# Router rows read back and turned on VectorE, expert tables read one expert ahead, routing by counted rivals

## The chip, the cores and the metric

The kernel runs on one core of one Trainium2 chip. The metric is the time of one execution on the device, in microseconds. Everything is computed in float32.

## The reference, cut to what matters

Two layers run over 2048 tokens of 1024 channels. Each layer adds a mixer (sliding-window attention, pooling and retention behind one RMS norm), and then a mixture of 32 experts behind a second RMS norm. The router takes the two best experts inside the best of eight groups of four.

```python
def moe_ffn(h, router_w, router_b, w_gate, w_up, w_down):
    ...
    scores = jax.nn.sigmoid(jnp.dot(hf, router_w))
    biased = (scores + router_b).reshape(t, N_EXPERT_GROUPS, EXPERTS_PER_GROUP)
    group_score = lax.top_k(biased, 2)[0].sum(-1)
    _, g_idx = lax.top_k(group_score, 1)
    in_group = jnp.take_along_axis(biased, g_idx[:, :, None], axis=1)[:, 0]
    _, local = lax.top_k(in_group, TOP_K)
    ...
for l in range(DEPTH):
    ...
    x = x + jnp.einsum('bse,ed->bsd', mix, w_out[l])
    x = x + moe_ffn(rms_norm(x, norm_ffn[l]), router_w, router_b, w_gate[l], w_up[l], w_down[l])
```

## The kernel before

**Two stages per layer.** The mixer stage goes through the 16 tiles of 128 tokens in a software pipeline of 18 steps (`steps`). In step s a tile s is projected (`front`), tile s-1 is mixed and its new x made (`back`), and tile s-2 is routed (`tail`). Steps 2 to 15 have all three parts, step 16 has `back` and `tail`, step 17 has `tail` alone. The expert stage then goes through the 32 experts in order of their load, with a fixed width of tokens for each (168 down to 128, `WIDTHS`), in groups of at most 32 tokens per quarter of the partitions (`GROUPS`: 6, 5 or 4).

**What sets the order.** Every engine has its own program, written out by hand; the engines meet at semaphores. The sync engine (SP) issues almost all direct DMAs in one queue of its own, in program order, and waits in that queue (`wait_alone`). GpSimd (POOL) issues the indirect DMAs: it scatters each tile's slots into `table` in DRAM, gathers the rows of an expert (L634), and adds the results into `out` (L641).

**The router in the mixer stage.** The new x of tile s-1 is finished on VectorE (DVE) at the end of step s (`x_new`, L966). SP stores it to `out` (L450). In the next step TensorE (PE) turns the eight 128x128 blocks of it into the PSUM banks bA and bB (`tr`, shown by the trace as part of L1154, semaphore `pe_h2T`), and DVE multiplies them by the norm's gain into `h2T` (L897, two instructions). PE then makes the router's partial products (L1275), ScalarE (ACT) copies them (`logits4`, L724), PE folds them (L1286), and ACT takes the exponential (L727). DVE runs `route`: it finds the best group and the two best experts with `first_of` (maximum, compare with a descending code, maximum, compare: L978 to L984), once on 8 groups and twice on 32 experts. PE counts ranks (L1198, L1199), and DVE's `place` writes the slots (L1033 to L1046).

**The final tile.** In step 17 nothing else is left to run. Its chain is PE's turns, DVE's L897, the norm (`norm_2`: L806 to L859, then the rows `h2n` by L864), `route`, ranks, `place`, the scatter, the table's first rows (L471, L472), their gather (L618) and PE's turns of those rows (L1366).

**The expert stage.** For expert i, SP waits for the gate and up products of expert i-2 (`gu_done`), then reads expert i's part of the table (L491, four DMAs), and then starts its weights (L457, L463). POOL waits for that table (L629), issues the gathers of expert i, and then the adds of expert i-2; it waits until the adds have landed before it goes on. DVE's `x_in` turns the gathered rows of expert i+1 (L1099, L1102) before it makes the hidden values of expert i (L1132, L1134, L1137), which PE's down products (L1403) wait for. PE's gate and up products are L1375.

## Time and profile before

| | |
|---|---|
| median of 3 runs | 3338.16 us (3337.02 to 3342.19) |
| the profiled execution | 3337.25 us |
| its span in the trace | 3335.4 us (1.85 us lie around it) |
| PE matmul busy | 3189.2 us, 96% |
| DVE busy | 1535.5 us, 46% |
| POOL busy | 1233.5 us, 37% |
| ACT busy | 590.2 us, 18% |
| mean granted TensorE clock | 0.978 |

The span begins with layer 0's mixer stage (to about 889 us) and its expert stage (to about 1660 us), and layer 1 follows in the same way (mixer to about 2551 us, experts to the end). A fully staffed mixer step takes about 50.7 us, an expert 21.4 to 27.4 us. Of the 146 us in which no matmul runs, most lie at the seams: at the end of each layer's mixer stage, between the two layers, and at the start and the end.

### The profile page before, as it was taken

The page shows a single profiled execution, that of the slowest core. Times are in us where ns is not written, and L with a number is a line of the kernel's source. Part 1 is how long each engine was busy: PE and PEld are TensorE (multiplying, and loading weights), DVE is VectorE, ACT ScalarE, POOL GpSimd, SP SyncE. Part 2 cuts the span into 40 slices and gives each one's busy share as a digit, 9 for nine tenths or more (in the row PEclk, how much of TensorE's full clock was granted, in tenths as well). Part 3 has the DMA queues.
Part 4 walks back from the last instruction along what each step waited for, and adds up shares of the span by engine and source line. Part 5 has one row for each costly group of instructions (what it writes and reads, how often), then busy time and mean ns, then how long its engine had stood idle before and what let it go on. Part 6 is the DMA issues. An engine that isn't in the chain of part 4 may idle for free.

```text
span 3335.4 us, 60077 instructions
## 1 busy us (share of the span) xinstructions
PE 3189.2 (96%) x20372; PEld 2502.4 (75%) x20372; DVE 1535.5 (46%) x4768; ACT 590.2 (18%) x1746; POOL 1233.5 (37%) x1346
## 2 busy tenths in 40 slices
PE   7999999999699999999889999999986999999998
PEld 4556556565499999999845565565555999999998
DVE  3676676776322222222236776766763222222221
ACT  2222122222011111111122222221220111111111
POOL 1221321322155555554321322212212555555543
PEclk9999999999799999999989999999987999999999
DMA  7212112122388999999842122121124889999996
GB/s 274 70 35 70 55 49 70 42 64 93 142 272 286 318 311 338 330 335 340 284 143 70 36 69 70 35 70 61 44 111 152 254 289 315 304 342 337 333 347 190
DMA packets 228594, 612.83 MB, mean 184 GB/s; under 512 B 63724, under 2 KB 120556, under 8 KB 195516
## 3 DMA queue, kind: packets, MB, share of 16 engines
q1 hardware_dynamic: 165724, 526.77, 43.5%
q0 software_dynamic: 62592, 82.75, 11.4%
q8 instruction: 126, 2.06, 0.2%
q14 instruction: 152, 1.25, 0.1%
HBM read 530.18 MB, written 80.35 MB: 183 GB/s over the span
## 4 chain that ended last, share of the span: by engine, by line
PE 87%; DMA 4%; DVE 3%; issue 3%; SPq 2%; DVEq 1%; POOL 1%; ACT 1%; ACTq 0%; POOLq 0%
PE bank L1375 25%; PE bank L1187 18%; PE bank L1403 15%; PE bank L1343 13%; PE bank L1183 3%; PE bank L1180 3%; PE bank L1154 3%; DMA arena<-hrows,arena 2%; PE bank L1299 1%; PE bank L1320 1%; PE bank L1249 1%; DVE arena L1099 1%; PE bank L1258 1%; PE bank L1275 0%; DMA arena<-in_x 0%
## 5 line engine op out<-in xcount | busy, mean ns | idle before, releaser
L1375 PE MATMUL bank<-arena,wts 128*128 128x135 f32 (+6 forms) x8192 | 1023.4, 287 | 3.3 <-ACTq L764 3.3
L1375 PEld LDWEIGHTS bank<-arena,wts 128*128 128x128 f32 x8192 | 1017.1, 191 | 3.4 <-issue 3.4
L1187 PE MATMUL bank<-wts,arena 128*128 128x512 f32 x1536 | 694.7, 599 | 37.9 <-DVE arena L847 20.8
L641 POOL DMA_INDIRECT out<-arena x316 | 501.6, 1587 | 158.1 <-issue 88.1
L1187 PEld LDWEIGHTS bank<-wts,arena 128*128 128x128 f32 x1536 | 281.3, 191 | 341.0 <-issue 320.9
L1403 PE MATMUL bank<-arena,wts 128*128 128x135 f32 (+6 forms) x4096 | 518.6, 287 | 15.7 <-DVE arena L1132 15.5
L1403 PEld LDWEIGHTS bank<-arena,wts 128*128 128x128 f32 x4096 | 510.9, 191 | 18.6 <-issue 18.2
L1343 PE MATMUL bank<-wts,arena 128*128 128x512 f32 x1024 | 453.6, 596 | 0.3 <-DVE arena L940 0.2
L1099 DVE STREAM_TRANSPOSE arena<-arena 128x256 f32<-128x256 f32 x304 | 135.5, 446 | 555.5 <-DMA arena<-hrows,arena 535.5
L1343 PEld LDWEIGHTS bank<-wts,arena 128*128 128x128 f32 x1024 | 192.5, 191 | 231.2 <-issue 214.8
L634 POOL DMA_INDIRECT arena<-hrows,arena x304 | 294.4, 968 | 183.3 <-issue 162.6
L537 POOL TENSOR_TENSOR arena<-arena 128x256 f32<-128x256 f32 x32 | 23.1, 722 | 847.7 <-DVEq L935 847.7
L1113 DVE STREAM_TRANSPOSE arena<-bank 128x480 f32<-128x480 f32 (+4 forms) x192 | 104.2, 594 | 473.6 <-PE bank L1403 473.6
L771 ACT ACTIVATE arena<-arena,tab 128x256 f32<-128x256 f32 x316 | 133.0, 496 | 616.2 <-DVEq L1114 616.2
L596 POOL DMA_INDIRECT table<-pay,sloti x64 | 63.7, 995 | 330.4 <-DVE sloti L1046 302.0
L629 POOL TENSOR_TENSOR arena<-tab,quarter 128x5 int32<-128x5 int32 (+2 forms) x64 | 12.2, 191 | 426.3 <-DMA tab<-table 400.6
L1183 PEld LDWEIGHTS bank<-arena,wts 128*128 128x128 f32 x1024 | 154.5, 191 | 13.1
L1183 PE MATMUL bank<-arena,wts 128*128 128x128 f32 x1024 | 155.5, 274 | 0.0
L1180 PE MATMUL bank<-wts,arena 128*128 128x256 f32 x512 | 153.1, 381 | 0.0
L779 ACT ACTIVATE arena<-bank 128x270 f32<-128x270 f32 (+6 forms) x64 | 26.3, 411 | 650.1 <-PE bank L1375 650.1
L1154 PEld LDWEIGHTS bank<-cst,arena 128*128 128x128 f32 x896 | 103.9, 144 | 44.0 <-issue 38.6
L1154 PE MATMUL bank<-cst,arena 128*128 128x128 f32 x896 | 126.4, 283 | 1.6 <-DVE arena L966 1.6
(184 smaller groups left out, 2768.7 us busy)
## 6 DMA issues: line engine op xcount, KB each, us to landing
wts<-in_w_gate SPq DMA_DIRECT2D x128, 1024.0 KB, 8.3
wts<-in_w_up SPq DMA_DIRECT2D x128, 1024.0 KB, 11.2
wts<-in_w_down SPq DMA_DIRECT2D x128, 1024.0 KB, 14.8
hrows<-arena SPq DMA_DIRECT2D x36, 512.0 KB, 3.0
out<-arena SPq DMA_DIRECT2D x36, 512.0 KB, 3.2
arena<-in_x SPq DMA_DIRECT2D x32, 512.0 KB, 4.8
wts<-in_w_in SPq DMA_DIRECT2D x8, 2048.0 KB, 16.3
arena<-out SPq DMA_DIRECT2D x32, 512.0 KB, 4.3
```

The lines of the kernel that those rows point to most:

```text
L634: e.indirect_dma_start(xg[b][:, g * PIECE:(g + 1) * PIECE], None, hpieces, bass.IndirectOffsetOnAxis(ap=piece[:, i, g:g + 1].bitcast(U32), ...
L641: e.indirect_dma_start(opieces, bass.IndirectOffsetOnAxis(ap=piece[:, i, g:g + 1].bitcast(U32), axis=0), ysb[b][:, g * PIECE:(g + 1) * PIE ...
L771: a(y, y, ACT.Copy, scale=tab[:, i, g, 1:2].bitcast(F32)).then_inc(y_scaled, 1)
L1099: v.transpose(windows(xT_all[b], g * step, DC, 32 * GMAX, 32), x_piece)
L1113: v.transpose(y[:, 3 * k:3 * k + m], windows(bk, 0, m, w, w))
L1154: return nc.tensor.transpose(dst, src, ident[0:m, 0:m])
L1180: mm(bIP1[:, 0:256], hT[:, d], win[:, 1, d, 0:256], start=(d == 0), stop=(d == DC - 1), skip_group_check=True)
L1183: i = mm(bIP1[:, 256 + P * j:384 + P * j], win[:, 1, d, 256 + P * j:384 + P * j], hT[:, d], start=False, stop=(d == DC - 1), skip_group_ch ...
L1187: i = mm(bIP[n % 2][:, :], hT[:, d], win[:, n, d], start=(d == 0), stop=(d == DC - 1))
L1343: i = mm(bIP[k][:, :], dT[o][:, d - 4] if d in (4, 5) else mixT[:, d], wout[:, d, 512 * k:512 * k + 512], start=(n == 0), stop=(n == DC - 1))
L1375: return mm(gu_at(f, k, w), lhs, xT[:, d, 0:w], start=start, stop=(d == DC - 1), skip_group_check=True)
L1403: j = mm(dst, lhs, hTm[:, f, 0:w], start=(f == 0 and d % 3 == 0), stop=(f == FC - 1), skip_group_check=True)
```

## The change

Four edits, which the diff below shows in cut form.

- **The router's rows.** For every tile but a layer's last, SP reads the stored x back from `out` in four DMAs, one for each quarter of the channels, into `hq`; `hq` is the same memory as `xT`, so SP first waits for `hT_ready` (the last reader of `xT`), and for `x_stored` (the store just issued). DVE turns `hq` in 32x32 blocks into `h2T` with one instruction. The channels then lie in the order of `by_quarters`, and the gain is multiplied into the router's weights once a layer. PE's eight turns and the wait `pe_h2T` in SP's queue are gone from these steps.
- **The final tile** keeps PE's turns, as 32 products with an identity that put the channels in the new order; DVE copies one half of the result and ACT the other. ACT's exponential waits for `r2_ready`, which DVE gives before it makes `h2n`.
- **Routing.** Each expert's rivals inside its group are counted (greater, or equal and ahead), and an expert is picked when fewer than two beat it and its group is the best. The first-of on 8 groups stays.
- **Tables.** SP reads the table of expert i+1 before the weights of expert i; expert 1's before expert 0's. POOL gathers the rows of expert 1 without waiting for expert 0's table, which it needs only for its adds.

```diff
@@ SP, step
                         if tail:
                             wait_alone(e, x_stored, (t0 - 1) * 16)
-                            wait_alone(e, pe_h2T, t0 - 1)
                         load_x(xr[b], xr_full[b], s)
...
                     if back:
                         wait_alone(e, x_new, t0 * 2)
                         e.dma_start(out[rows(s - 1), :], xr[1 - b]).then_inc(x_stored, 16)
+                        if front:
+                            wait_alone(e, hT_ready, t0 + 2 if has_next(s) else t0 + 1)
+                            wait_alone(e, x_stored, t0 * 16)
+                            for a in range(4):
+                                e.dma_start(hq[32 * a:32 * a + 32, :].rearrange("p (g c) -> p g c", g=4),
+                                            out[rows(s - 1), PIECE * a:PIECE * a + PIECE].rearrange("(g s) c -> s g c", g=4)).then_inc(hq_full, 16)
@@ SP, expert
-                        index = i if i == 0 else e.value_load(order[0:1, i:i + 1], ...)
-                        slot = e.snap(index * STRIDE + r * w)
+                        slot = e.snap(r * w)
                         wait_alone(e, gu_done, n * 2 + 2)
...
-                        for a in range(4):
-                            e.dma_start(tab[...], table[bass.ds(slot, w), :]...).then_inc(tab_full[b] if i else tabq_in, 16)
+                        if i < NE - 1:
+                            following = e.value_load(order[0:1, i + 1:i + 2], ...)
+                            load_table(i + 1, e.snap(following * STRIDE + r * WIDTHS[i + 1]), tab_full[(i + 1) % 4])
                         if i == 0:
+                            load_table(0, slot, tabq_in)
...
                         else:
-                            load_weights(index, b, n)
+                            load_weights(e.value_load(order[0:1, i:i + 1], ...), b, n)
@@ POOL, gather and add
                         if i == 0:
                             gather_rows(turn)
-                        if i == 0:
-                            wait_alone(e, tabq_in, turn * 64 + 64)
-                        else:
-                            wait_alone(e, tab_full[b], ...)
-                        e.tensor_tensor(piece[:, i, 0:GROUPS[i]], tab[:, i, 0:GROUPS[i], 0], quarter[:, 0:GROUPS[i]], ALU.add)
+                            return
+                        wait_alone(e, tab_full[i % 4], ...)
+                        pieces(i)
...
                     def add(i, b, w):
+                        if i == 0:
+                            wait_alone(e, tabq_in, turn * 64 + 64)
+                            pieces(0)
@@ ACT, step
                     if tail:
+                        if not (front or back):
+                            e.wait_ge(pe_h2T, l + 1)
+                            a(h2T[:, 4:8], bB[:, :]..., ACT.Copy).then_inc(h2T_half, 1)
                         e.wait_ge(pe_parts, t0 - 1)
                         a(logits4, bA[:, 0:P], ACT.Copy).then_inc(parts_read, 1)
-                        e.wait_ge(h2n_ready, t0 - 1)
+                        e.wait_ge(r2_ready, t0 - 1)
@@ DVE
+                v.tensor_tensor(rw, rw, bc(gffn8.unsqueeze(2), [P, DC, NE]), ALU.mult)
...
                     if tail:
-                        e.wait_ge(pe_h2T, t0 - 1)
-                        for k in range(2):
-                            v.tensor_tensor(h2T[:, 4 * k:4 * k + 4], (bA, bB)[k]..., bc(gffn[...]), ALU.mult)
+                        if front or back:
+                            e.wait_ge(hq_full, (l * (TILES - 1) + s - 1) * 64)
+                            v.transpose(h2T.rearrange("p d (g n) -> p g d n", g=4), hq)
+                        else:
+                            e.wait_ge(pe_h2T, l + 1)
+                            v.tensor_copy(h2T[:, 0:4], bA[:, :].rearrange("p (d n) -> p d n", d=4))
                         e.drain().then_inc(h2T_ready, 1)
@@ DVE, route (each of the four new instructions on 128 values stands beside an old one, before the same drain)
+                    v.tensor_tensor(rivals[:, :, :, 4:8], other, own, ALU.is_equal)
...
+                    v.tensor_tensor(rivals[:, :, :, 0:4], other, own, ALU.is_gt)
...
+                    v.tensor_tensor(rivals[:, :, :, 4:8], rivals[:, :, :, 4:8], bc(const("ahead")...), ALU.mult)
...
+                    v.tensor_reduce(losses, rivals.rearrange("p g j k -> p (g j) k"), X, ALU.add)
                     e.drain()
                     first_of(g8[0], 8, stat[:, 2:3], g8[3], const("rev8"))
-                    v.tensor_scalar(g8[4], g8[3], 1.0, BIG, ALU.subtract, ALU.mult)
-                    v.tensor_tensor(mb..., bi..., bc(g8[4]...), ALU.add)
-                    first_of(mb, 32, stat[:, 2:3], oh1, const("rev32"))
-                    v.scalar_tensor_tensor(out=mb2, in0=oh1, scalar=-BIG, in1=mb, op0=ALU.mult, op1=ALU.add)
-                    first_of(mb2, 32, stat[:, 2:3], oh2, const("rev32"))
-                    v.tensor_tensor(pick, oh1, oh2, ALU.add).then_inc(picks_ready, 1)
+                    v.scalar_tensor_tensor(out=by_group(pick), in0=by_group(losses), scalar=2.0, in1=hot,
+                                           op0=ALU.is_lt, op1=ALU.mult).then_inc(picks_ready, 1)
+                    for k, oh in enumerate((oh1, oh2)):
+                        v.scalar_tensor_tensor(out=by_group(oh), in0=by_group(losses), scalar=float(k), in1=hot,
+                                               op0=ALU.is_equal, op1=ALU.mult)
@@ PE, step
-                    if tail:
+                    if tail and not (front or back):
                         e.wait_ge(x_new, (t0 - 1) * 2)
                         for d in range(DC):
-                            i = tr((bA, bB)[d // 4][:, (d % 4) * P:(d % 4) * P + P], xr[b][:, d * P:(d + 1) * P])
+                            dst = (bA, bB)[d // 4][:, (d % 4) * P:(d % 4) * P + P]
+                            for a in range(4):
+                                at = a * PIECE + d * 32
+                                i = mm(dst[32 * a:32 * a + 32], xr[b][:, at:at + 32], ident, start=True, stop=True)
```

In `place` the update of `tok` also moves behind the slots' cast.

The order of PE in a fully staffed step, from the attention's and retention's score products (L1249 to L1262) to the projection's second chunk (L1180, L1183), before:

```order
L1249 MATMUL bank<-arena 128x128 x8
L1258 MATMUL bank<-arena 128x128 x4
L1262 MATMUL bank<-arena 128x64 x4
L1265 REGISTER_ALU
L1154 MATMUL bank<-cst,arena 128x128 x8
L1175 REGISTER_ALU
L1180 MATMUL bank<-wts,arena 128x256
```

and after:

```order
L1283 MATMUL bank<-arena 128x128 x8
L1292 MATMUL bank<-arena 128x128 x4
L1296 MATMUL bank<-arena 128x64 x4
L1209 REGISTER_ALU
L1214 MATMUL bank<-wts,arena 128x256
```

The eight turns are gone and nothing takes their place on PE. In SP's queue, from the store of the new x to the store of the normalised rows, before:

```order
L450 DMA out<-arena 128x1024
L324 ISA
L428 DMA hrows<-arena 128x1024
```

and after:

```order
L455 DMA out<-arena 128x1024
L330 REGISTER_ALU x2
L460 DMA arena<-out 32x4x256
L460 ISA
L460 DMA arena<-out 32x4x256
L460 ISA
L460 DMA arena<-out 32x4x256
L460 ISA
L460 DMA arena<-out 32x4x256
L330 ISA
L434 DMA hrows<-arena 128x1024
```

Two waits (the rows at L330) and four reads now stand ahead of everything that SP issues for the next step. In SP's queue for one expert of the expert stage (`TENSOR_LOAD order` reads an expert's number into a register), before:

```order
L483 TENSOR_LOAD order
L483 ISA x2
L324 ISA
L491 ISA
L491 DMA tab<-table 28x6x2 x4
L457 ISA
L457 DMA wts<-in_w_gate 128x2048
```

and after:

```order
L330 ISA
L507 TENSOR_LOAD order
L507 ISA x2
L484 ISA
L484 DMA tab<-table 28x6x2 x4
L516 TENSOR_LOAD order
L516 ISA x2
L468 ISA
L468 DMA wts<-in_w_gate 128x2048
```

The table that is read is now the next expert's, and both register loads stand behind the wait (`ISA` at L330) and ahead of the weights, where one stood ahead of the wait (`ISA` at L324).

## Rows read from the trace of the kernel before

**Rows 1.** The page, part 1: busy time of TensorE over the span.
```profile
PE 3189.2 (96%) x20372; PEld 2502.4 (75%) x20372; DVE 1535.5 (46%) x4768; ACT 590.2 (18%) x1746; POOL 1233.5 (37%) x1346
```
**Rows 2.** Windows: one mixer step. Window, length, busy by engine, clock, DMA share, GB/s.
```profile
560.30:611.00 50.70, 50.70 (x246) 29.83 (x245) 35.91 (x124) 11.99 (x39) 12.87 (x21) 1.00 0.18 57
```
**Rows 3.** Timeline of PE in that step: start, length, what; each product is two records.
```profile
569.21 1.09 PE L1154 MATMUL bank<-cst,arena 128*128 128x128 f32 x8
570.14 0.60 PE L1180 MATMUL bank<-wts,arena 128*128 128x256 f32 x2
...
577.26 0.64 PE L1275 MATMUL bank<-arena,par 128*32 128x128 f32 x16
577.83 3.70 PE L1187 MATMUL bank<-wts,arena 128*128 128x512 f32 x8
581.37 0.38 PE L1284 MATMUL bank<-arena,cst 128*128 128x128 f32 x2
```
**Rows 4.** Timeline of DVE in that step.
```profile
559.42 0.69 DVE L966 TENSOR_TENSOR arena<-arena,bank 128x512 f32<-128x512 f32 x1 [0.55 <-PE bank L1343]
...
572.24 1.29 DVE L897 TENSOR_TENSOR arena<-bank,par 128x512 f32<-128x512 f32 x2 [0.19 <-issue]
```
**Rows 5.** The page, part 6: DMA issues, KB each, median us to landing.
```profile
out<-arena SPq DMA_DIRECT2D x36, 512.0 KB, 3.2
...
arena<-out SPq DMA_DIRECT2D x64, 128.0 KB, 4.0
```
**Rows 6.** Line L390, the quarter reads from `out`: their landing.
```profile
DMA to landing us min/median/max: 2.8/4.0/15.3
```
**Rows 7.** Timeline of ACT in that step.
```profile
571.29 1.06 ACT L672 ACTIVATE arena<-arena 128x1024 bf16<-128x1024 f32 x1 [8.60 <-DMA arena<-in_x]
...
578.00 0.28 ACT L724 ACTIVATE arena<-bank 128x128 f32<-128x128 f32 x1
```
**Rows 8.** Timeline of PE in steps 16 and 17 and at the expert stage's start.
```profile
826.19 1.08 PE L1275 MATMUL bank<-arena,par 128*32 128x128 f32 x16 [2.34 <-DVEq L899]
...
854.21 1.09 PE L1154 MATMUL bank<-cst,arena 128*128 128x128 f32 x8 [0.78 <-DVE arena L966]
...
883.83 4.09 PE L1366 MATMUL bank<-cst,arena 128*32 128x128 f32 x128 [10.98 <-DMA arena<-hrows,row]
```
**Rows 9.** Timeline of DVE in step 17, the norm's end and routing.
```profile
860.80 0.18 DVE L990 TENSOR_SCALAR arena<-arena 128x32 f32<-128x32 f32 x1 [0.35 <-ACT arena L727]
...
864.06 0.17 DVE L1009 TENSOR_SCALAR arena<-arena 128x8 f32<-128x8 f32 x1
...
867.65 0.18 DVE L1020 CUSTOM_DVE_ANT_0 arena<-arena 128x32 f32<-128x32 f32 x1
```
**Rows 10.** Timeline of DVE in the mixer step: one form on 128 values, and the next.
```profile
580.63 0.29 DVE L827 TENSOR_SCALAR arena<-cst,stat 128x128 f32<-128x128 f32 x1
580.84 1.24 DVE L842 STREAM_TRANSPOSE arena<-arena 128x1024 f32<-128x1024 f32 x1
```
**Rows 11.** Timeline of PE: the down products of expert 0, layers 0 and 1.
```profile
912.25 9.36 PE L1403 MATMUL bank<-arena,wts 128*128 128x168 f32 x64 [2.55 <-DVE arena L1132]
...
2575.93 11.04 PE L1403 MATMUL bank<-arena,wts 128*128 128x168 f32 x64 [4.10 <-DVE arena L1132]
```
**Rows 12.** Windows: the narrow experts, one of six windows, and the six's sum.
```profile
3170.00:3270.00 100.00, 99.79 (x893) 99.59 (x892) 25.28 (x53) 12.39 (x34) 51.76 (x44) 1.00 1.00 348
sum 600.00, PE 591.35 PEld 589.36 DVE 152.20 ACT 77.44 POOL 324.03; mean PE 98.56 PEld 98.23 DVE 25.37 ACT 12.91 POOL 54.00
```
**Rows 13.** Timeline of POOL at expert 1.
```profile
893.43 0.20 POOL L629 TENSOR_TENSOR arena<-tab,quarter 128x6 int32<-128x6 int32 x1 [11.67 <-DMA tab<-table]
```
**Rows 14.** Waits of the span: us in total, times, longest.
```profile
POOL arena L629 <- DMA tab<-table: 400.6, 57, 11.9
...
POOL arena L629 <- DMA out<-arena: 25.6, 5, 5.7
```
**Rows 15.** Line L457, gate and up weights, 1480 to 1600 us: their landing.
```profile
DMA to landing us min/median/max: 5.2/10.1/14.5
```

More of the change, by code:

```diff
@@ L102, in constant_arrays @@
     put("token", i)
+    put("ahead", np.tile((np.arange(4)[None, :] < np.arange(4)[:, None]).reshape(1, 16), (P, 1)))
     put("quarter", np.tile(i // 32, (1, GMAX)))
@@ L209, in program @@
         xr = [part("mix", D) for _ in range(2)]
-        xT, hT = (part("mix", D).rearrange("p (d n) -> p d n", d=DC) for _ in range(2))
+        hq, hT = part("mix", D), part("mix", D).rearrange("p (d n) -> p d n", d=DC)
+        xT = hq.rearrange("p (d n) -> p d n", d=DC)
         proj = [part("mix", DIN) for _ in range(2)]
@@ L235, in program @@
         mixT = part("mix", D).rearrange("p (d n) -> p d n", d=DC)
-        es, sc, bi, mb, mb2 = (part("mix", 32) for _ in range(5))
+        es, sc, bi, losses = (part("mix", 32) for _ in range(4))
         r32, oh1, oh2, pick, slots, junk = (part("mix", 32) for _ in range(6))
@@ L315, in groups_to, with tables_to @@
             return sum(GROUPS[:i])
+        def tables_to(i):
+            return sum(1 for k in range(1, i + 1) if k % 4 == i % 4)
         def lane_gathers_to(i):
@@ L610, in _, with pieces @@
                     turn = e.snap(turns)
+                    def pieces(i):
+                        e.tensor_tensor(piece[:, i, 0:GROUPS[i]], tab[:, i, 0:GROUPS[i], 0], quarter[:, 0:GROUPS[i]], ALU.add)
+                        e.drain()
                     def gather_rows(turn):
@@ L1273, in step @@
                         e.wait_ge(h2T_ready, t0 - 1)
+                        if not (front or back):
+                            e.wait_ge(h2T_half, l + 1)
                         for d in range(DC):
```

45 lines of the change are left out of this document (25 added, 20 removed).

## The prediction

> **What bounds the kernel now.** I read the page's busy times first: TensorE is busy 3189 us of a span of 3335 [rows 1]. So an edit pays if it takes work from PE where PE is packed, or a wait from PE where it stands. Second, windows over single mixer steps: in 50.7 us PE is busy 50.7, DVE 35.9, the DMA engines 18% [rows 2]. PE alone sets a fully staffed step, and all others have room. Third, PE's timeline in that step, which says what each group costs in pitch, and the timelines of DVE and ACT beside it, for the deadlines [rows 3, 4, 7]. Fourth, the same at the seams, steps 16 and 17, where PE waits [rows 8, 9]. Last the expert stage: PE is packed but for waits in front of the down products, each for DVE's L1132, and DVE is late because it turned expert i+1's rows first and had waited for them [rows 11, 12].
>
> **The mixer steps.** The eight turns start at 569.21 and the next group at 570.14 [rows 3]: 0.93 us of PE's time (the row's own 1.09 overlaps). PE has no idle time in the step, so the 0.93 is on the path. It goes in steps 2 to 15 of both layers, 28 times: 26.0 us. In step 16 it pays nothing: PE waits there 2.34 us for DVE's L897 anyway [rows 8], and its successor, DVE's turn of 1.24 us (form of L842 [rows 10]) against 1.29 for L897 [rows 4], is ready at the same moment.
>
> That holds if the read-back is in time. Count from x_new, 560.11 (L966's end [rows 4]). The store is issued at once and lands in 3.2 us [rows 5]; SP then issues four reads, some 1.9 us for all by the four quarter reads of the same step, the last 1.4 us in, and it lands 4.0 us later [rows 5, 6]. With some tenths for the waits the rows are there 9.0 us after x_new. DVE comes to the turn at 12.1 (572.24 [rows 4]), so no wait; done at 13.5. PE wants `h2T` at L1275, 577.26 less the 0.93 now saved, 16.2 after x_new [rows 3]. The cover is 2.8 us beyond DVE's turn. SP's later issues: the normalised rows are ready only 5.0 us after x_new, and the queue is free at 5.3, so the next tile's x is late by 0.3 us, and up to 1.7 more if it shares bandwidth with the 0.5 MB added (about 300 GB/s). ACT waits for that x at 571.29, and everything up to L724 hangs on it [rows 7]; L724 would end at 579 to 580, and PE wants it ahead of L1284 at 580.4 (581.37 less 0.93) [rows 3]. Cover 0.4 us at worst, so I take nothing, and hold a small loss for the range. DVE's own step becomes shorter by routing (below), off the path.
>
> **The seam at the end of each mixer stage** is a chain of single steps, so every edit counts, twice.
> - Turns by 32 products instead of 8. The trace has no such group on a warm clock. L1275 has eight products of this form in 0.57 us from start to start [rows 3], so 32 take 2.3, against 0.93: +1.4. The upper bound is L1366, 4.09 us for 64 such products at the lower clock [rows 8]: +3.2. The lower bound is no loss at all. I take +1.4, the nearest form.
> - The evacuation: DVE's two instructions (1.29 [rows 4]) become one of half the size, ACT has the other: -0.6. Bounds 0 and -0.6.
> - `r2_ready`: DVE waits 0.35 us for ACT's exponential [rows 9]; it is now asked for 0.75 us earlier: -0.35.
> - Routing. From L1009 to L1020 3.59 us go [rows 9]. Added: four instructions on 128 values that share a drain with an old one, 0.21 each by the pitch of L827 [rows 10], 0.85; and three small ones, two undrained, about 0.65. Net -2.1. Bounds -2.6 (the four hidden entirely) and -1.0 (each with its full 0.29 and a drain).
> - `tok` behind the cast: -0.1.
>
> Sum -1.75 a layer, so -3.5 us; bounds 0 and -5.4. The router weights' gain (0.4 us, once a layer) lies under DVE's wait for the first x and w_in. 
>
> **The expert stage.** The table of expert 1 is read only after x is turned, so POOL waits 11.7 us for it [rows 13], its gathers start at 894, and PE stands at expert 0's down products 2.55 us in layer 0 and 4.10 in layer 1, where the clock then falls (11.04 us against 9.36 for the same 64 records [rows 11]): 8.3 us in all. Read first, the table lets POOL gather at about 883, 11 us earlier, and all 8.3 go. Expert 1's weights are then issued some 1 us later, with 5 us or more to spare.
>
> For the later experts POOL waited 57 times for a table, 401 us [rows 14]. Six windows of 100 us over the narrow experts show PE busy 591.35 of 600 [rows 12]: 8.65 us lost. With tables an expert ahead POOL waits for its own adds to land, 5.1 us (25.6 in 5 [rows 14]), where it now waits 4.6 to 9.1. For experts of width 135 its cycle is 2.0 + 5.1 + 1.2 + 9.1 + 5 = 22.4 us (address, gathers, adds, landing) against PE's 22.1: no spare, but gathers start 1 to 4 us earlier. At width 128 it is 19.5 against 21.4. I take the 8.65 as gone, with 0 and 12.6 as bounds: 12.6 is what the starts of L1375 give, 16 narrow experts a layer against their undisturbed length.
>
> SP now loads two registers behind its wait, at some 1.2 us each, so weights are issued about 2.4 us later. Gate and up weights land at the latest 14.5 us after issue [rows 15], in about 19 us of the 28.6 that the double buffer gives. That is covered.
>
> **The sum.** 26.0 + 3.5 + 8.3 + 8.65 = 46.5. The profiled execution took 3337.25, span 3335.4 and 1.85 around it; 3337.25 - 46.5 = 3290.8. The median stands 0.9 higher: 3291.7, and I say 3291.
>
> **The rivals.**
> - A. The gathers stay late at the narrow experts. For it: POOL's cycle of 22.4 against 22.1, and a DMA share of 1.00 with PE at 99.8% [rows 12]. Against it: the throughput falls to a third once an expert, so the queues do run empty. Expert 0's 8.3 still go; 3291 + 8.65 = 3300.
> - B. The step doesn't shrink as PE's work does: ACT's late x holds PE at L1284 by most of the 0.93. For it: cover of 0.4 us at worst. Against it: the added reads fall mostly in an idle stretch of the DMA engines, before the normalised rows. 3291 + 26 = 3317.
> - C, slower than before. The read-back comes late, on the same queue as 2.25 MB of other traffic, and PE waits at L1275. It costs from 14.9 us after x_new (16.2 less 1.3), where I expect 9.0; each us beyond costs 28 us, and the gain is gone at 16.6. The slowest quarter read on record landed after 15.3 us [rows 6]; were that the rule, the rows would be there at 20.2, 5.3 x 28 = 148 us: 3439. Against it: the median is 4.0, and the slow ones stood beside the loads of w_in and w_out at a layer's start.
> - D. The change does more: the 12.6, the seam's bound, and a POOL that runs ahead: 3281.
> - E. The turns' removal is hidden, as at step 16, in all steps: the time of B, by another way; the packed PE of [rows 2] excludes it almost.
>
> **How the numbers follow.** The forecast, 3284 to 3297, 0.68. A 0.14, B and E 0.08, C 0.04, D 0.06. Its range 3282 to 3306 holds the forecast, A and half of D: 0.85, a little wide for the unknown seam. A measurement can tell 0.2% (6.7 us) from no change; below 3331.5 lie the forecast, A, B, D and E, above 3345 lies C; a mix of B with half of C would land between: faster 0.93, same 0.03, slower 0.04.
>
> **What would show it.** Right: mixer steps of 49.8 us in PE's timeline with no turns; DVE's turn of `hq` without a wait; L1275 and L1284 without a wait; DVE's chain from L990 to the first weighted sum shorter by 2 us; no wait of L1403 at expert 0; POOL's wait for `tab` gone and one for its adds in its place. Wrong: a wait of DVE for `hq`, of PE for ACT's logits, of L1403 at the narrow experts (A), or of L1375 for weights, which I count as covered.

## The result: 18 us where 46 were forecast

| | time, us (5 runs) | ratio to before |
|---|---|---|
| before, run beside it | 3340.9 (3337.0 to 3342.2) | |
| changed | 3320.8 (3318.0 to 3323.4) | 0.9944 [0.9933, 0.9955] |
| forecast | 3291 (3282 to 3306) | |

The changed kernel is faster, by 18 us between the two profiled executions (3337.25 and 3319.35), not by 46.5, and the time lies outside the range. One execution of before_fixed, below, took 8628 us and is left out of its ratio.

**The page after**, part 1 (busy time, share, instructions) and lines of part 6 (KB each, median us to landing), beside [rows 1, 5]:
```profile
PE 3165.6 (95%) x20244; PEld 2477.4 (75%) x20244; DVE 1517.5 (46%) x4578; ACT 588.9 (18%) x1748; POOL 1242.0 (37%) x1346
...
arena<-out SPq DMA_DIRECT2D x184, 128.0 KB, 3.2
...
arena<-in_x SPq DMA_DIRECT2D x32, 512.0 KB, 6.1
```
PE does 23.6 us less work, and the read-back lands quickly; but the loads of whole tiles of x, 4.8 us before, now take 6.1.

**Where the time went.** The landmarks are PE's turns x10 that open a mixer step (from one opening to the next is a pitch) and the first and last down products of a layer. Forecast and measured, both layers:

| stretch | forecast | measured |
|---|---|---|
| steps, 14 + 15 pitches: 712.65 + 764.97 before, 705.98 + 759.38 after | -26.0 | -12.3 |
| last step's opening to expert 0's down products: 98.79, 100.56; 93.57, 93.83 | -10.15 | -11.95 |
| first to last down products: 739.95, 738.27; 741.62, 742.85 | -10.3 | +6.25 |
| the rest | 0 | 0 |

(The forecast's 8.3 at expert 0 is split: 6.65 of waits in the second line, 1.68 of clock in the third.) Layer 0's 14 pitches are steps 2 to 15; layer 1's 15 begin with step 1, which routes nothing and takes 52.5 us before and after. So there are two errors, of 14 and 17 us.

**A mixer step after**, windows (columns as [rows 2]) and PE's timeline (as [rows 3]):
```profile
554.90:605.70 50.80, 50.30 (x238) 28.88 (x236) 35.27 (x119) 11.91 (x38) 12.74 (x20) 1.00 0.22 67
```
```profile
555.01 1.26 PE L1188 MATMUL bank<-cst,arena 128*128 128x128 f32 x10
...
572.22 0.65 PE L1314 MATMUL bank<-arena,par 128*32 128x128 f32 x16
576.33 0.38 PE L1323 MATMUL bank<-arena,cst 128*128 128x128 f32 x2
...
605.68 1.28 PE L1188 MATMUL bank<-cst,arena 128*128 128x128 f32 x10 [0.50 <-DVEq L1078]
615.78 0.46 PE L1292 MATMUL bank<-arena 64*128 64x128 f32 x3 [0.86 <-DVE arena L899]
```
PE, never idle in this step before, now waits, and not where I had looked: the router's products (L1314) and the logits' sum (L1323) come without a wait, but the next step's opening waits 0.50 us for DVE's `place` and its retention scores 0.86 for the copy of `rT`. The steps that have no such wait take 49.91 us, the others up to 51.3. SP, ACT and DVE in the same step (as [rows 4, 7]; SP's second line is the same load in the kernel before):
```profile
562.82 0.33 SPq L380 DMA_DIRECT2D arena<-in_x  x1
...
566.58 0.35 SPq L374 DMA_DIRECT2D arena<-in_x  x1
```
```profile
570.14 1.06 ACT L694 ACTIVATE arena<-arena 128x1024 bf16<-128x1024 f32 x1 [11.66 <-DMA arena<-in_x]
```
```profile
568.04 1.25 DVE L925 STREAM_TRANSPOSE arena<-arena 128x1024 f32<-128x1024 f32 x1 [0.21 <-issue]
574.78 0.17 DVE L942 TENSOR_TENSOR stat<-stat 128x8 f32<-128x8 f32 x1 [2.75 <-ACT stat L735]
...
605.51 0.17 DVE L1079 CAST sloti<-arena 128x2 int32<-128x2 f32 x1
605.65 0.68 DVE L996 TENSOR_TENSOR arena<-arena,bank 128x512 f32<-128x512 f32 x1
610.47 0.75 DVE L892 TENSOR_SCALAR arena<-arena,stat 128x1024 f32<-128x1024 f32 x1
614.94 0.69 DVE L899 COPY arena<-bank 128x512 f32<-128x512 f32 x1 [3.73 <-issue]
```
Read it downwards. DVE's turn of `hq` has no wait for the read-back. The next tile's x reaches ACT 14.2 us after x_new (555.9); before it was 11.2 ([rows 7] less 560.11). So the exponentials end late, DVE stands 2.75 us for them and then works with only short gaps to the end of `place` at 605.65, which delays the second half of x_new. Then comes 3.73 us in front of the `rT` copy in which DVE waits for nothing that the trace names.

This is one of the steps with a later x. Over the 26 steps in which ACT waits for it, x comes 13.2 us after x_new in the median (11.6 to 14.8); in the kernel before it came at 11.5 (10.2 to 13.0). The same waits over the span (us in total, times, longest), three of the kernel before, then three of the changed one:
```profile
PE bank L1258 <- DVE arena L871: 5.6, 7, 2.1
DVE arena L871 <- issue: 24.2, 10, 2.5
DVE stat L912 <- ACT stat L713: 11.1, 11, 5.1
...
PE bank L1188 <- DVEq L1078: 3.4, 8, 0.5
DVE arena L899 <- issue: 32.7, 10, 3.9
DVE stat L942 <- ACT stat L735: 42.1, 23, 4.8
```
So the kernel before had the late exponentials and the wait for `rT` already, in small. Of its steps 2 to 15 in both layers, 18 took 50.73 to 50.77 us and ten 51.06 to 51.29; the step of [rows 2] is one of the 18.

**The experts after**, PE's timeline (as [rows 11]), one window (as [rows 12]), and the waits of PE and POOL over the span (us in total, times, longest; as [rows 14]; the first line is the kernel before):
```profile
901.11 4.16 PE L1442 MATMUL bank<-arena,wts 128*128 128x168 f32 x28
...
1332.62 7.62 PE L1442 MATMUL bank<-arena,wts 128*128 128x135 f32 x64 [2.05 <-DVE arena L1166]
...
2553.07 4.15 PE L1442 MATMUL bank<-arena,wts 128*128 128x168 f32 x28
```
```profile
3170.00:3270.00 100.00, 98.59 (x882) 98.39 (x881) 22.20 (x48) 11.84 (x32) 50.91 (x45) 1.00 1.00 351
```
```profile
PE bank L1403 <- DVE arena L1132: 15.5, 12, 4.1
...
PE bank L1442 <- DVE arena L1166: 14.9, 14, 2.5
...
PE bank L1314 <- DVEq L929: 10.2, 4, 4.3
PE bank L1292 <- DVE arena L899: 9.7, 10, 2.1
```
```profile
POOL arena L631 <- DMA out<-arena: 361.7, 58, 8.7
```
Expert 0 no longer waits, in either layer. At the narrow experts PE waits 14 times, 14.9 us; before it was 15.5 less the 6.65 at expert 0, so 8.9. And POOL now stands 6.2 us per expert (361.7 by 58) for its own adds to land where it stood 7.0 for a table.

### The profile page after: what moved, and what is told of

It reads as the page before. It is cut to its first block, busy times and chain, and to the rows that moved or that the text cites. A ratio compares the mean times of both kernels' runs of the same rounds, so it can differ in the third digit from the quotient of the medians.

```text
span 3317.4 us, 59849 instructions
## 1 busy us (share of the span) xinstructions
PE 3165.6 (95%) x20244; PEld 2477.4 (75%) x20244; DVE 1517.5 (46%) x4578; ACT 588.9 (18%) x1748; POOL 1242.0 (37%) x1346
## 4 chain that ended last, share of the span: by engine, by line
PE 69%; DVE 8%; DMA 8%; issue 6%; DVEq 4%; SPq 2%; ACT 2%; POOL 1%; ACTq 0%; POOLq 0%
PE bank L1414 24%; PE bank L1442 15%; PE bank L1221 12%; PE bank L1382 9%; DMA arena<-hrows,arena 2%; PE bank L1214 2%; PE bank L1217 2%; DMA out<-arena 2%; DMA arena<-in_x 2%; PE bank L1188 1%; DMA arena<-out 1%; ACT arena L733 1%; DVE arena L1133 1%; PE bank L1338 1%; PE bank L1359 1%
## 5 line engine op out<-in xcount | busy, mean ns | idle before, releaser
L1414 PE MATMUL bank<-arena,wts 128*128 128x135 f32 (+6 forms) x8192 | 1023.5, 287 | 3.2 <-ACTq L789 3.2
L1414 PEld LDWEIGHTS bank<-arena,wts 128*128 128x128 f32 x8192 | 1017.1, 191 | 3.4 <-issue 3.4
L1442 PE MATMUL bank<-arena,wts 128*128 128x135 f32 (+6 forms) x4096 | 518.6, 287 | 15.0 <-DVE arena L1166 14.9
L631 POOL TENSOR_TENSOR arena<-tab,quarter 128x5 int32<-128x5 int32 (+2 forms) x64 | 12.2, 191 | 363.9 <-DMA out<-arena 361.7
L775 ACT ACTIVATE arena<-arena 128x1024 bf16<-128x1024 f32 x32 | 33.8, 1057 | 447.7 <-DVE arena L996 447.7
L1188 PEld LDWEIGHTS bank<-cst,arena 128*128 128x128 f32 x640 | 74.3, 143 | 44.5 <-issue 44.4
```

What stands on the lines that cost most here:

```text
L1188: return nc.tensor.transpose(dst, src, ident[0:m, 0:m])
L1414: return mm(gu_at(f, k, w), lhs, xT[:, d, 0:w], start=start, stop=(d == DC - 1), skip_group_check=True)
L1442: j = mm(dst, lhs, hTm[:, f, 0:w], start=(f == 0 and d % 3 == 0), stop=(f == FC - 1), skip_group_check=True)
```

## The experiments

They came back in five groups, from different chips: the kernel before took 3341 us beside some, 3366 to 3370 or 3401 beside others, and there the later experts start up to 24.3 us apart instead of 22, waiting for weights. So each ratio holds within its own group, and what is compared across groups is the mixer's pitches and, with care, the us from first to last down products. Packed pitches are the same on every chip (49.91 and 50.74). Pitches with waits in them are not: eight traces have the changed kernel's mixer (after, after_again, adds_later, adds_later_2, old_tables, old_tables_2, pool_both, no_drain), and their steps 2 to 15 of both layers sum to 1406.9 to 1416.6 us. A difference of a few us between two such traces says little.

| run | before | ratio, 95% | pitches, layers 0 and 1 | first to last down |
|---|---|---|---|---|
| x_early | 3401 | 0.9865 [.985, .988] | 702.5, 754.7 | 757.0, 757.8 |
| before_x_early | 3401 | 0.9983 [.9974, .9992] | 713.3, 765.8 | 768.0, 769.4 |
| adds_later | 3401 | 0.9901 [.9886, .9916] | 704.5, 764.4 | 758.6, 760.0 |
| old_tables | 3401 | 0.9941 [.9927, .9954] | 708.5, 760.6 | 769.7, 768.5 |
| after_again | 3341 | 0.9935 [.9922, .9949] | 705.6, 756.6 | 743.0, 745.4 |
| rT_first | 3341 | 0.9901 [.9885, .9916] | 701.2, 753.5 | 744.1, 743.2 |
| adds_later_2 | 3341 | 0.9914 [.9901, .9928] | 706.5, 757.4 | 737.9, 740.2 |
| all_three | 3341 | 0.9852 [.9837, .9867] | 698.7, 751.2 | 737.9, 740.0 |
| old_tables_2 | 3370 | 0.9937 [.9924, .995] | 703.1, 756.4 | 753.8, 755.6 |
| reads_only | 3370 | 1.0046 [1.0033, 1.0059] | 721.5, 774.8 | 753.2, 753.0 |
| four | 3370 | 0.9792 [.9779, .9804] | 698.7, - | 733.4, 732.2 |
| before_fixed | 3370 | 0.9966 [.9954, .9979] | 710.3, 762.8 | 750.6, 754.1 |
| old_routing | 3366 | 1.0003 [.9994, 1.0012] | 716.9, 767.2 | 744.4, 745.0 |
| x_early_2 | 3366 | 0.9907 [.9892, .9922] | 702.1, 754.4 | 747.6, 748.1 |
| pool_both | 3366 | 0.9859 [.9844, .9874] | 705.9, - | 733.4, 733.7 |
| before_four | 3366 | 0.9979 [.997, .9988] | 710.3, - | 748.6, 750.0 |
| four_2 | 3369 | 0.9785 [.9771, .9798] | 698.7, - | 733.7, 733.7 |
| no_drain | 3369 | 0.9914 [.99, .9927] | 706.9, - | 745.0, 745.0 |

(-: a record is missing at that layer's first pitch.)

**x_early, x_early_2, before_x_early: the load of x ahead of the read-back.**
```diff
-                            load_x(xf, xf_full, s + 1)      # behind the normalised rows
+                    if front and (not isinstance(s, int) or s < TILES - 2):
+                        wait_alone(e, sumsq_f, t0 + 2)
+                        load_x(xf, xf_full, s + 2)          # ahead of SP's wait for x_new
...
                         a(squares, xr[o], ACT.Square, accum_out=stat[:, 4:5]).then_inc(sumsq_2, 1)
+                        e.drain()                           # on ACT
```

> Changed kernel, with the load of x for the sum of squares issued one tile further ahead on SP's queue, before the wait for x_new and so before the store and the four reads back. Theory 1 (late x): in the changed kernel this load lands 14.2 us after x_new instead of 11.2, ACT's exponentials end late, DVE's weighting of the probabilities waits 2.75 us for them, and DVE's chain then comes late for PE. With x early all pitches of steps 2 to 15 fall to 49.9 us: 14 pitches of layer 0 from 706.0 to about 699, 15 of layer 1 from 759.4 to about 751.5, in all 13 to 15 us less, 3306 to 3308, 0.990 of the kernel before. Theory 2 (DVE is too full or slowed by POOL, whenever x lands): pitches stay at 50.4 on average, 3321, 0.994. Theory 3 (the read-back's traffic itself holds PE back, through another landing): as theory 2, with waits on a DMA.

> Kernel before, with the same early load of x. Theory 1: its steps are 50.73 where packed, and 14 pitches of layer 0 sum to 712.65, 2.4 more than 14 times that; these extras go, 2 to 3 us a layer, 4 to 6 in all, 3335, 0.9985. And the difference to the changed kernel with x early is then what the removed turns are worth in themselves: 28 x 0.82 to 0.93 = 23 to 26 us of steps, beside seam and expert 0. Theory 2: extras stay, no change, 3341.

> Changed kernel with x early, again, for its ratio on a chip where the weights don't set the pace. Its pitches were 8.1 us shorter in sum than the changed kernel's (3.5 and 4.7): 3312 where the kernel before takes 3341, 0.991. If the clear of late x at the layer's start counts too, 0.990.

ACT's wait for x went, and of DVE's for the exponentials 4.4 us in 2 are left, but the pitches fell by 8.2 and 8.9 us where 15.4 were to be had, and every second step still took 50.3 to 50.9. (Against old_tables and pool_both, which ran beside them with the changed kernel's mixer, they fell by 11.9 and 8.3.) What is left in x_early's steps is one wait of PE:
```profile
PE bank L1297 <- DVE arena L904: 8.2, 10, 1.9
```
Ten times is once for each time that the loop over pairs of steps goes back, five a layer, and just there DVE stood 30.6 us (32.7 in the changed kernel, 24.2 before) with nothing named. The trace's DMA records add something: in all 20 cases, before and changed, a packet of 8 KB on the instruction queue (q14) starts inside this idle time, 2.0 to 2.4 us ahead of the copy. So DVE seems to wait there for its next instructions; no run tests it. The late x is half of the answer. In the kernel before the same edit didn't shorten the pitches; its 0.17% is not explained.

**rT_first: the copy of `rT` ahead of norm_2**, out of the way of the loop's edge.
```diff
                         if front:
+                            e.wait_ge(pe_qkrT, t0 + 1)
+                            v.tensor_copy(rT..., bE[:, :]).then_inc(rT_ready, 1)   # the old copy stays for step 1 alone
                             norm_2(s, o)
```

> Changed kernel, with DVE's copy of the turned retention queries (rT) moved ahead of norm_2, into the 1.2 us in which DVE waits for ACT's sum of squares. Theory 1 (every second step DVE stands 3.3 to 3.8 us at the loop's back edge in front of that copy, 32.7 us in 10, and PE waits 9.7 us for it): these 9.7 us of PE's wait go, and the waits L1188 stay: 8 to 10 us less than the changed kernel. Theory 2 (what is late is DVE's whole chain, from the exponentials on): the copy comes before norm_2, but the next DVE work is later by the same amount, and PE waits at the inner products instead, 0 to 3 us gained.

It took 12.1 us less than after_again, where 8 to 10 were expected; the waits at the retention scores are gone from PE's list, and the pitches fell by 7.5. The rest of the 12.1 (3.4 lies ahead of layer 1's expert 0) I did not trace.

**adds_later: POOL's wait for landed adds behind the next gathers.**
```diff
                         gather(i, b, w)
+                        if i >= 3:
+                            landed(i - 3)
                         if i >= 2:
-                            add(i - 2, b, WIDTHS[i - 2])   # issued and landed
+                            add(i - 2, b, WIDTHS[i - 2])   # issued only
```

> Changed kernel, with POOL's wait for the landing of expert i-2's adds moved behind the gathers of expert i+1. Theory 1 (the gathers are late because POOL stands in that wait, 361.7 us in 58 waits): PE's waits before the down products for DVE's hidden product, 14.9 us in 14, go almost wholly, with the clock that one of them costs: 10 to 15 us less than the changed kernel, 3306 to 3311, 0.991. Theory 2 (the DMA engines are full at the narrow experts, share 1.00, and a gather issued earlier lands no earlier): the waits stay, 3321, 0.994. Theory 3 (gathers then queue ahead of the adds and the landing of adds becomes late for the turned y): PE's waits move, 3320 or worse.

> The changed kernel itself, beside the others on one chip. The first four experiments ran on a chip where the kernel before takes 3401 us and the later experts start 24.3 us apart instead of 22, so that none of them can be set against the changed kernel's 3321. If the expert stage is bound by the weights' arrival there, the changed kernel's ratio is 0.989 to 0.990 on such a chip (x early being worth 8 us in its steps: 3356 + 8), and 0.9944 on a chip where the kernel before takes 3340.

> Changed kernel with POOL's wait for its adds behind the next gathers, again, beside the changed kernel. If the chip is one where the kernel before takes 3340: 14.9 us of waits at the down products go, 10 to 15 us less than the changed kernel. If it is one where it takes 3401 and the weights set the pace: no gain from it, since nothing there waits for the gathers.

On the chip where the weights come slowly adds_later was 14 us behind x_early and says little. Beside after_again it took 7.5 us, half of what I expected: a wait of 9.7 us stayed in front of the down products. POOL's timeline there shows why:
```profile
1309.71 1.55 POOL L663 DMA_INDIRECT out<-arena  x1 [0.30 <-issue]
1310.71 1.36 POOL L631 TENSOR_TENSOR arena<-tab,quarter 128x5 int32<-128x5 int32 x1
1318.86 1.01 POOL L653 DMA_INDIRECT arena<-hrows,arena  x1 [6.79 <-issue]
```
The addresses are done right behind the adds, and the first gather starts 8 us later, with no named cause. All that stands between is a drain.

**four, all_three, pool_both, no_drain: that drain.**
```diff
-                        e.drain()
+                        # the add's own then_inc(piece_ready, 1), and here:
+                        wait_alone(e, piece_ready, turn * NE + (3 if i == 0 else i if i <= 2 else i + 1))
```

> Changed kernel with x early, the rT copy first and POOL's wait for its adds later. If the three causes are the whole of the shortfall, the steps 2 to 15 are 49.9 us each (14 pitches 699, 15 pitches 751.5, 15 us less than in the changed kernel) and the narrow experts lose at most 3 us of 600: 25 to 29 us less than the changed kernel, ratio 0.986 on a chip where the kernel before takes 3340. If x early and rT first remove the same waits twice, 20 us less, 0.9885.

> The kernel with x early, the rT copy first and the adds' wait later, and POOL's drain behind the piece addresses replaced by a wait on that instruction's own semaphore. In adds_later_2 the first gather starts 8.4 us after the addresses, 5 to 7 us after the start of the down products, though nothing that the program asks for is missing: the drain seems to wait until POOL's adds have landed. Theory 1 (it does): addresses to first gather take 1 us, gathers start 6 us earlier, x is turned 5 us earlier, and the last 9.4 us of PE's waits at the down products go: 3283, 0.983. Theory 2 (the wait is in the queue or the engines, which are full): gathers start or land as late as before, 3292, 0.985.

> Changed kernel with the adds' wait later and the drain replaced, the mixer untouched. Theory 1 (POOL's two waits for its landing adds are the narrow experts' whole loss): 742 us from the first to the last down products of a layer become 733, 17 to 19 us less than the changed kernel, 0.9885, and the mixer's steps keep their losses. Theory 2 (part of the gain of the four edits came through the mixer): 10 us less, 0.991.

> Changed kernel with the drain behind the piece addresses replaced by a wait on the instruction's own semaphore, and POOL's wait for its adds left where it is. Theory 1 (drain and explicit wait both stand until the adds have landed, so that either alone holds the gathers): no gain, the ratio of the changed kernel, 0.994, addresses to first gather 1.8 instead of 2.0 us. Theory 2 (the drain cost time of its own in every expert, and taking it away was the gain): 12 us less, 0.990.

> The changed kernel with all four edits, again, for its ratio on another chip. The first time, 0.979, ran where the kernel before takes 3370. On one where it takes 3340, 3280 to 3283, 0.982 to 0.983; where the weights are slower, 0.979 to 0.980.

POOL in `four`, at the same place in its order:
```profile
1431.68 1.55 POOL L667 DMA_INDIRECT out<-arena  x1 [0.30 <-issue]
1432.69 0.78 POOL L635 TENSOR_TENSOR arena<-tab,quarter 128x4 int32<-128x4 int32 x1
1434.49 1.02 POOL L657 DMA_INDIRECT arena<-hrows,arena  x1 [1.02 <-issue]
```
and a window over its narrow experts:
```profile
3060.00:3160.00 100.00, 100.00 (x886) 100.00 (x885) 26.93 (x53) 13.11 (x35) 54.77 (x44) 1.00 1.01 349
```
1.8 us instead of 8.2; DVE begins to turn the rows 9 to 12 us after the down products' start instead of 16 to 20 (adds_later_2), and in this window PE is never idle. With the mixer untouched (pool_both) the same 733 us come out, on chips that are slower than the first; its ratio is 0.9859, better than either theory had it.

no_drain alone kept 745 and POOL's explicit wait:
```profile
POOL arena L631 <- DMA out<-arena: 385.1, 58, 8.7
```
It saved 0.8 us an expert from addresses to gathers (1.2 for 2.0). Its ratio, 0.9914, lies between the two theories, and the changed kernel didn't run beside it; but old_routing, with drain and wait both in place on a chip of 3366, has the same 744.4 and 745.0 from first to last. So the drain stood for the landing a second time: in adds_later_2 the first gather starts 7.6 us after the last add's record ends (1311.26), and in the changed kernel POOL's explicit wait ends 7.2 us after it, at the same place in the order. And all_three has every pitch of steps 2 to 15 at 49.90 to 49.91: what the steps lost against packed ones was the late x and the loop's edge.

**reads_only, old_routing: the two halves of the mixer's change, each alone.** reads_only adds to the kernel before the store's read-back into an unused buffer, with DVE's wait for it; old_routing puts the two `first_of` over 32 experts back into the changed kernel.

> Kernel before, with the four quarter reads of the router's rows added, into a buffer that nobody uses; PE still turns the rows. Theory 1 (the 0.5 MB of the reads delays the next tile's x): in_x lands about 14 us after x_new instead of 11.2, ACT's sum of squares waits 11.7 instead of 8.6, DVE waits for the exponentials, and some steps grow by 0.2 to 0.5 us: 3 to 8 us slower, 3344 to 3349. Theory 2 (x is late in the changed kernel because of the queue's order alone, 0.4 us): x lands at 11.6, no change, 3341.

> Changed kernel with the old routing (first_of twice over 32 experts), all else as changed. Theory 1 (routing lies on the path at the seam alone): PE's wait for the picks in step 17 goes from 6.9 to 9.3 us a layer, 4.8 us more than the changed kernel, 0.996. Theory 2 (DVE's chain is the bound in many steps since x lands late there): DVE is 1.1 us longer between the logits and the sums in every step, and PE's waits for place (3.4 us in 8) and at the retention scores grow by 0.3 to 1.1 us in most of 28 steps: 12 to 25 us more than the changed kernel, 0.998 to 1.002.

The reads, with SP's two waits for them, cost the kernel before 8.8 and 9.8 us in its pitches, ratio 1.0046, 15 us where theory 1 had 3 to 8. x comes 13.5 us after x_new (median of 26 steps), as late as in the changed kernel, and DVE waits 42.2 us in 24 times for ACT's exponentials: theory 1's cause is right, its price was too low. And the routing that I had called off the path is worth 18.8 us of steps (716.9 + 767.2 against 706.0 + 759.4), 19.4 against pool_both, which ran beside it with the new routing (15 to 25 over the eight traces with that mixer). That is theory 2. With the old one PE waits for `place` in most steps:
```profile
PE bank L1185 <- DVEq L1075: 11.5, 21, 0.8
```
Without it the changed kernel is no faster than before: ratio 1.0003.

**old_tables, old_tables_2: the tables read in their own turn.**
```diff
-                            load_table(i + 1, ..., tab_full[(i + 1) % 4])
+                        load_table(i, slot, tab_full[b] if i else tabq_in)
```

> Changed kernel, with the tables read as before (expert i's table in expert i's turn, behind x_turned at expert 1). Theory 1 (reading ahead removed expert 0's stall and made the narrow experts a little worse, since POOL now meets its own adds): expert 0's waits of 2.6 and 4.1 us with the clock loss of 1.7 come back, +8.3, and the six windows of the narrow experts lose 8.7 instead of 13.5, -4.8: 3324 to 3325, 0.9955. Theory 2 (the narrow experts' loss has nothing to do with the tables): +8.3 alone, 3329, 0.9968.

> Changed kernel with the tables read as before, again, on a chip where the kernel before takes 3340 (the first time the weights set the pace). Theory 1 (reading ahead takes 8.3 us from expert 0 and gives 7.9 back at the narrow experts, 741.6 and 742.9 us from the first to the last down products against 740.0 and 736.6 without expert 0's clock loss): no net change against the changed kernel, 3320, 0.994. Theory 2 (the narrow experts' loss comes from elsewhere): 8 us more than the changed kernel, 3328, 0.996.

0.9937 where the changed kernel had 0.9935 and 0.9944 would be no net change, as theory 1 had it. But the chips differ (3370 against 3341), so this doesn't show it. On those of 3366 to 3370 us the layer's 32 experts take 751 to 756 with the old order (before_fixed, reads_only, old_tables_2) and 744 to 748 with the new, so there reading ahead pays. For theory 1's balance there is only the table of the first chip (+8 against -8.3), where the other edits ran along.

**before_fixed, before_four: the same covers given to the kernel before.**

> Kernel before, with x early and the rT copy first. Its steps should all be 50.73 to 50.74 us: 14 pitches 710.3 instead of 712.7, 15 pitches 762.8 instead of 765.0, 4.5 us less, 3336, 0.9985. Against the same two edits in the changed kernel (steps of 49.91) the removed turns are then worth 28 x 0.83 = 23.1 us. If the edits do more (the rT copy alone took 12 us from the changed kernel, its pitches only 7.5), 3330.

> Kernel before with all four edits: x early, the rT copy first, the adds' wait later, no drain. The difference to the changed kernel with the same four is what the change is worth where nothing else is late. Theory 1: 23.1 us of steps, about 6 of seams, 8.3 at expert 0, in all 37; on a chip of 3340 the four edits give 3282 in the changed kernel, so 3319 here, 0.9935. Theory 2 (with tables read in their own turn POOL waits for a table, not for its adds, so the two edits on POOL bring nothing here): 3330 to 3336, 0.9966 to 0.9985, and reading ahead is worth more than expert 0's stall, because it lets the other edits work.

before_fixed has all pitches of steps 2 to 15 at 50.73 or 50.74, so the turns are worth 0.83 us a step, 23.1 in 28. It gained 11 us, of which the pitches explain 4.5; the rest stays open. before_four kept 749 us per layer of experts where `four` needs 733: moving the adds' wait and the drain brings little while POOL waits for its table. The change with all four edits against the kernel before with them: 0.9792 against 0.9979, some 63 us at 3370, of which 23 in the steps and 33 in the experts. `four` beats both kernels: 0.9785 and 0.9792.

## Why the prediction was wrong, step by step

Two terms failed. The mixer's steps gave 12.3 us of 26.0: the prediction took nothing for the next tile's late x, since it followed it only to ACT's logits, and held DVE off the path. The narrow experts lost 6 us more where 8.65 were to go: POOL's wait for its own adds took longer than the five cases from which it was priced.

- **PE's turns, 28 x 0.93.** That PE alone sets a fully staffed step was read in one step; in the kernel before ten of the 28 were 0.3 to 0.6 us longer, which its trace had, and before_fixed, without the late x and the loop's edge, has none of it. The price was a little high: packed steps are 49.91 against 50.735, 0.83 each, 23.1. Read back in time: right, DVE never waited for `hq`, and rival C is dead.
- **"The next tile's x is late by 0.3 us, and up to 1.7 more."** In the step shown it was 3.0 late: SP issued it 0.4 later (6.9 us after x_new for 6.5), but behind the read-back's 0.5 MB it landed 7.3 us after issue instead of 4.7. Over the 26 steps it was 1.7 late in the median (issue 0.6, landing 1.1), which is inside the prediction's 2.0, though 17 of the 26 come later than the latest of before. So the lateness was sized about right; what it meets was not.
- **"I take nothing", the cover of 0.4 us at L1284.** I had followed the late x to one successor, ACT's logits. They were in time. **The step that failed** stood beside it: ACT's exponentials. In the kernel before they end at 575.89 in this step and DVE asks for them at 576.19 (L912), a cover of 0.3 us. Behind that wait comes the whole of DVE's chain to `place`, x_new and `rT`, which has little idle time left. "All others have room" [rows 2] was read from a busy share. By windows of DVE, from x_new to L942 and from there to the next x_new, it is in the changed kernel (length, DVE busy, clock, DMA share, GB/s)
```profile
555.90:574.78 18.88, 9.53 (x27) 1.00 0.58 181
574.78:605.65 30.87, 25.00 (x91) 1.00 0.00 0
```
half idle ahead of the wait and four fifths busy behind it, where even the rest is the gaps between dependent instructions. With the loop's edge this took 10.9 of the 23.1 us (the steps stand 15.4 above packed ones, and 4.5 of that was lost in the kernel before too). reads_only, x_early and rT_first show both causes. Rival B was the nearest, by another wait; that the measured 3320.8 lies near its 3317 is luck, as B has the whole loss in the steps.
- **"DVE's own step becomes shorter by routing, off the path."** This is the same failed step seen from the other side: DVE is on the path, so its shorter routing is worth 18.8 us, more than the 12.3 that the steps gained in all. And that with a small saving, smaller than at the seam: from the first instruction of routing to L970 the step takes 9.95 us for 11.06 before, 1.1 less and not 2.1, since the same instructions take longer there. L1031, a comparison of 128 values, once in the step and once at the seam:
```profile
586.95 0.82 DVE L1031 TENSOR_TENSOR arena<-arena 128x128 f32<-128x128 f32 x1
...
2507.99 0.28 DVE L1031 TENSOR_TENSOR arena<-arena 128x128 f32<-128x128 f32 x1
```
In the step POOL works beside DVE, at the seam it doesn't. In the same step L1036, of the same size, took 0.28 us at 588.98, just as POOL paused (from 589.03 to 589.36). The Trainium skill, GPSIMD Engine Reference, section Architecture, has the Pool engine's read and write ports to SBUF shared with DVE; that agrees, but no run here took POOL away.
- **The seam, -3.5.** -2.5 and -2.6 a layer from the turns' start to the first gate product, -5.0. By terms:
```profile
2500.11 1.96 PE L1304 MATMUL bank<-cst,arena 128*32 128x128 f32 x64 [0.78 <-DVE arena L996]
2502.91 0.64 PE L1314 MATMUL bank<-arena,par 128*32 128x128 f32 x16 [0.84 <-DVEq L929]
2503.95 0.41 PE L1325 MATMUL bank<-cst,arena 128*128 128x32 f32 x2 [0.40 <-ACT arena L749]
2511.30 0.64 PE L1232 MATMUL bank<-arena,cst 128*128 128x32 f32 x2 [6.94 <-DVE arena L1048]
```
The 32 products took 1.96 us against 1.09 [rows 8]: +0.87, not +1.4, nor the 3.7 us that the prediction had worked out by the rule. (The rule, column tiling and transpose mode excluding each other, is in the Trainium skill, TensorEngine Tiling (Array Packing), Gotcha 2. The trace disagrees with the 3.7; whether the exclusion holds, no run shows.) Logits to picks (L1325 to L1232) 7.35 us for 9.62 in layer 1 and 10.02 in layer 0 (L1286 to L1198 before): -2.3 and -2.7, forecast -2.45. The terms of layer 0: +0.3 from the turns' start to the router's products (forecast +0.8), -2.7 for routing, +0.4 for `place`, -0.5 for the table and its gather. The prediction's bounds, 0 and -5.4, were no sum of its items' bounds, which come to +3.5 and -7.3.
- **Expert 0, -8.3.** Right: its waits of 2.55 and 4.10 us are gone, and its 64 records take 9.3 us in both layers.
- **Narrow experts, -8.65, and rival A.** The rival named the mechanism, but as "the loss stays", and its cycle of 22.4 us took 5.1 for the adds' landing, from five early waits [rows 14]. In 58 waits it is 6.2 on the mean and up to 8.7, so the same sum gives 23.5 and more against PE's 22.1, and the loss grows. pool_both, without the two waits, keeps 0.8 us of PE's 14.9. And the argument for A, a DMA share of 1.00, was no cause: `four` loses nothing at a share of 1.01, and gathers land 5 to 7 us after their last issue in the changed kernel, in adds_later_2 and in `four` alike.
- **Weights issued later:** covered, as forecast; no wait of L1414 but the first of each layer. The two register loads, priced at 1.2 us each, take 0.8 and 1.0 in the one expert that I read.

Forecast and result meet once the covers exist: all_three, with POOL's drain still in place, takes 3292.6 us beside a kernel before of 3341. That is chance in part, since it carries three edits more.

## What to carry to other kernels

Read more than one step before you call an engine the only bound. A busy share is not slack: follow a transfer that comes late to every instruction that it feeds, on every engine, to the point where each is wanted, and look at where in the period the idle time lies. A wait that ends last hides the next one on the same queue, a drain among them, so price a removed wait by the successor's measured time under load, not by a quiet stretch. Ask of each "off the path" edit what the kernel would take without it; here the one part priced at nothing carried the gain.

## What the runs showed of the hardware

- A drain on POOL behind indirect adds stood until they had landed: 8.2 us from the addresses to the first gather (adds_later_2), 1.8 with a semaphore in its place (`four`).
- DVE stands 2.4 (before) to 3.3 us (after) at each return of a loop whose body is two mixer steps, 10 times in 10. In each a packet of 8 KB on the instruction queue starts 2.0 to 2.4 us before DVE goes on.
- A 512 KB load behind four reads of 128 KB took 6.0 us from issue to use in the median of 26 steps (the changed kernel, and reads_only too) where it took 4.9 before, 7.3 for 4.7 in the step shown.
- The kernel before took 3341 to 3401 us on different chips, 1.8% apart. For adds_later and adds_later_2, one program on two chips and 60.0 us apart, 40.5 us lie between first and last down products, 12.8 between the last step's opening and the first of them, 5.0 in the steps. Packed pitches agree to 0.01 us.
- An operation on 128x128 values on DVE (L1031) took 0.82 us in the step, with POOL busy, and 0.28 at the seam, with POOL idle.
